# The second FFN rearranged, and the four weight sums of a tile made by VectorE

## What is computed

```python
D_MODEL = 1024
D_FF = ((8 * D_MODEL // 3 + 127) // 128) * 128   # 2816
def swiglu(x, w1, w3, w2):
    return (jax.nn.silu(x @ w1) * (x @ w3)) @ w2
x = x + 0.5 * rmsnorm(swiglu(rmsnorm(x, norm_g[4]), ffn2_w1, ffn2_w3, ffn2_w2), norm_g[5])
```

## Time and profile before

| what | us |
|---|---|
| median of 3 runs (lowest, highest) | 1102.76 (1102.58, 1103.33) |
| the profiled execution | 1100.35 |
| its span, first to last instruction | 1098.5 |
| PE busy | 1056.8 (96%) |
| DVE busy | 652.5 (59%) |
| ACT busy | 411.9 (37%) |
| POOL busy | 161.8 (15%) |

### The profile page before, as it was taken

The page is one execution under the profiler, slowest core; times in us unless marked ns, Lnnn a source line. Parts: engine busy times, 40 slices in busy tenths (PEclk is TensorE's granted clock), DMA queues, the critical chain, the costliest instruction groups (busy, mean ns, idle before and its releaser), DMA issues. The chain is left out here.

```text
span 1098.5 us, 21180 instructions
## 1 busy us (share of the span) xinstructions
PE 1056.8 (96%) x8729; PEld 1040.3 (95%) x8729; DVE 652.5 (59%) x1072; ACT 411.9 (37%) x650; POOL 161.8 (15%) x209
## 2 busy tenths in 40 slices
PE   8999999999999999999999999968999989999998
PEld 7999999999999999998999999968999989999997
DVE  6534433433333379784577778756883588368746
ACT  6322124222122345321447544433552255234432
POOL 0000716910000000520000000041320122022100
PEclk9999999999999999999999999979999999999999
DMA  7222322223222240223411152221323133312222
GB/s 255 78 95 77 96 77 96 82 90 92 81 77 95 72 140 22 75 78 119 138 59 58 40 175 88 96 67 49 115 93 111 30 116 123 94 41 91 82 73 82
DMA packets 31509, 99.40 MB, mean 90 GB/s; under 512 B 3780, under 2 KB 6212, under 8 KB 31304
## 3 DMA queue, kind: packets, MB, share of 16 engines
q1 hardware_dynamic: 31432, 98.33, 27.7%
HBM read 93.58 MB, written 4.74 MB: 89 GB/s over the span
## 5 line engine op out<-in xcount | busy, mean ns | idle before, releaser
L1304 DVE TENSOR_TENSOR wl<-raw,wh 128x1024 fp32r<-128x1024 f32 (+2 forms) x117 | 135.6, 1159 | 264.3 <-ACT wh L705 263.6
L705 ACT CAST wh<-raw 128x1024 fp32r<-128x1024 f32 (+2 forms) x117 | 114.3, 978 | 312.2 <-PE ps L2489 250.4
L2489 PE MATMUL ps<-xh,wh 128*128 128x272 f32 x1040 | 218.4, 291 | 13.1 <-DVE wl L1304 12.0
L2489 PE MATMUL ps<-xl,wh 128*128 128x272 f32 x1040 | 216.1, 289 | 0.0
L2489 PE MATMUL ps<-xh,wl 128*128 128x272 f32 x1040 | 215.6, 289 | 0.0
L2489 PEld LDWEIGHTS ps<-xh,wh 128*128 128x128 f32 x1040 | 164.1, 190 | 14.6 <-DVE wl L1304 12.9
L2489 PEld LDWEIGHTS ps<-xl,wh 128*128 128x128 f32 x1040 | 164.9, 190 | 0.0
L2489 PEld LDWEIGHTS ps<-xh,wl 128*128 128x128 f32 x1040 | 163.8, 190 | 0.0
L2720 PE MATMUL ps<-hh,wh 128*128 128x272 f32 x304 | 63.4, 290 | 7.1 <-DVE wl L1304 7.0
L2489 PE MATMUL ps<-hh,wh 128*128 128x272 f32 x304 | 63.2, 289 | 0.3 <-DVE hl L1325 0.3
L2720 PE MATMUL ps<-hl,wh 128*128 128x272 f32 x304 | 62.8, 288 | 0.0
(11 more groups left out here) (572 smaller groups left out, 2421.5 us busy)
## 6 DMA issues: line engine op xcount, KB each, us to landing
raw<-w SPq DMA_DIRECT2D x66, 512.0 KB, 3.6
pair<-w SPq DMA_DIRECT2D x36, 512.0 KB, 4.5
raw<-win SPq DMA_DIRECT2D x25, 512.0 KB, 3.7
raw<-w SPq DMA_DIRECT2D x32, 384.0 KB, 3.2
raw<-wout SPq DMA_DIRECT2D x8, 512.0 KB, 4.0
raw<-w SPq DMA_DIRECT2D x12, 256.0 KB, 2.7
o_yT<-x SPq DMA_DIRECT2D x8, 272.0 KB, 2.2
cs<-cT SPq DMA_DIRECT2D x4, 516.0 KB, 4.7
```

Of the source, the lines that this page charges most:

```text
L705: nc.scalar.copy(wh[par][:, 0:cols], raw[par][:, 0:cols]).then_inc(hi_done, 1)
L1304: V.tensor_tensor(wl[par][:, 0:cols], raw[par][:, 0:cols], wh[par][:, 0:cols].bitcast(F32), ALU.subtract).then_inc(split_done, 1)
L2489: last = mm(ps[:, bank + s, 0:HALF], w[:, kk * P:(kk + 1) * P], a[:, kk, s * HALF:(s + 1) * HALF], start=(kk == 0 and i == 0), stop=(kk == ...
```

## The change

Three things are rearranged and one moves between engines. (1) `sums` moves from the raw buffers to the unused fourth slots of `base_hi` and `base_lo`. With it d0 and d1 of a part are loaded in the part's first tile, and the sums and splits of the next part's first tile are made among the down units. The load of a pair now also waits for `g_lo`. (2) At the head, the split of u0+6 goes ahead of `normed`, that of u0+7 ahead of the forms, and forms and bases are spread over the down units of part 0, whose results ACT copies out (`down_copy`) in place of DVE. (3) PE does d1's last four k-tiles, not one, behind the last of d0. (4) All four sums of a tile are made by DVE (`sum_2`, `sum_4`); POOL's loop goes. In the tile loop DVE's `lo_4` and `lo_a22` move back, the latter behind `lo_3(j+1)`.

Cut to its core, indentation and renamed slices left out. The down units of part 0 get, on ACT, d2, copy 0, base 1, d3, copy 1, base 2, d4, copy 2, form 6, d5, copy 3, hi_3, hi_a22, d6, hi_4, copy 4, d7 and so on, and the like on DVE with `sum_13(0)`, `sum_2(0)` behind d4. In parts 1 and 2 DVE has sum_13, sum_2 ahead of d2 and sum_4, lo_3, lo_a22 behind it.

```diff
-        sums = sb("sums", [P, 4 * KHP], at=raw_at)
+        sums = sb("sums", [P, 2, KD * T], at=xh_at + 12 * FORM)
...
@@ SyncE: load_pair, ffn2
                     spe.wait_ge(a22_lo, j - 1)
+                    spe.wait_ge(g_lo, j - 1)
                     spe.wait_ge(s4_sum, j - 1)
...
                 load_pair(0)
-                load_pair(1)
...
-                    if p:
-                        for j in range(N6 * (p - 1), last):
-                            if j + 2 < NG:
-                                load_pair(j + 2)
-                        spe.wait_ge(s12_lo, last + 1)
-                        spe.wait_ge(s3_lo, last + 1)
+                    for j in range(N6 * (p - 1), N6 * p) if p else ():
+                        if j + 2 < NG:
+                            load_pair(j + 2)
+                        if j % N6 == 0:
+                            down(0)
+                            down(1)
+                    if p == 0:
                         down(0)
-                        spe.wait_ge(s4_lo, last + 1)
                         down(1)
-                        if last + 2 < NG:
-                            load_pair(last + 2)
-                    for m in range(2 if p else 0, KD):
+                        load_pair(1)
+                    for m in range(2, KD):
                         down(m)
@@ ScalarE: hi_form, new helpers, ffn2
-                act.wait_ge(form_raw, i + 1)
+                act.wait_ge(form_raw, min(i + 1, 4))
...
+            def hi_base(i, src):
+                act.wait_ge(unit_used, down_unit(0, 0) + 2)
+                nc.scalar.copy(base_hi_t[:, i], src).then_inc(form_hi, 1)
+            def down_copy(m):
+                act.wait_ge(unit_used, down_unit(0, m) + 3)
+                act.wait_ge(form_lo, (4, 4, 5, 5, 7, 7, 7, 7)[m])
+                nc.scalar.copy(halves(y[:, m, :]), pair(down_set(0) + 2 * (m % 2))).then_inc(y_evac, 1)
...
                 up_split(u0 + 6)
+                up_split(u0 + 7)
                 silu(hb + 2, 0)
                 hi_form(0, form_hi_t[:, 2], form_t3[:], 1.0)
-                hi_form(1, form_hi_t[:, 0], xn[:, 0, 1], 1.0)
-                hi_form(2, form_hi_t[:, 1], form_t24[:], -1.0)
-                hi_form(3, form_hi_t[:, 3], form_t24[:], 1.0)
-                up_split(u0 + 7)
                 hidden_hi(hb + 2, 0, 2)
...
                         down(0)
+                        hi_form(1, form_hi_t[:, 0], xn[:, 0, 1], 1.0)
                         silu(hb + 3, 1)
+                        hi_form(2, form_hi_t[:, 1], form_t24[:], -1.0)
                         down(1)
+                        hi_base(0, xn[:, 0, 0])
                         hidden_hi(hb + 3, 1, 3)
...
@@ ScalarE, tile loop of parts 1 to 3
-                            hi_4(j)
-                            hi_a22(j)
-                            if j > j0:
-                                silu_pair(j - 1)
-                            keep_p1(j)
...
+                        if j > j0:
+                            hi_4(j)
+                            silu_pair(j - 1)
+                        keep_p1(j)
...
+                            hi_g(j + 1)
+                        if j > j0:
                             hi_a22(j)
+                        keep_p5(j)
+                        keep_u2(j)
...
@@ VectorE: sums
+            def sum_2(j):
+                dve.wait_ge(s13_sum, j + 1)
+                V.tensor_tensor(s2_raw, s1_raw, pairs[j % 2][:, A11B], ALU.add).then_inc(s2_sum, 1)
+            def sum_4(j):
+                dve.wait_ge(s2_sum, j + 1)
+                if j:
+                    dve.wait_ge(s4_lo, j)
+                V.tensor_tensor(s4_raw, s2_raw, pairs[j % 2][:, A12B], ALU.add).then_inc(s4_sum, 1)
@@ VectorE: ffn2, head
                 hidden_lo(hb + 1, 1, 1)
+                up_lo(u0 + 6)
                 for kk in range(KD):
                     normed(kk)
-                up_lo(u0 + 6)
                 up_first(hb + 2, 0, u0 + 4)
-                lo_form(0, form_lo_t[2][:], form_t3[:], form_hi_t[:, 2], 1.0)
-                lo_form(1, form_lo_t[0][:], xn[:, 0, 1], form_hi_t[:, 0], 1.0)
-                lo_form(2, form_lo_t[1][:], form_t24[:], form_hi_t[:, 1], -1.0)
+                up_lo(u0 + 7)
                 scaled(hb + 2, 0)
-                lo_form(3, form_lo_t[3][:], form_t24[:], form_hi_t[:, 3], 1.0)
-                up_lo(u0 + 7)
...
                         down(0)
+                        lo_form(0, form_lo_t[2][:], form_t3[:], form_hi_t[:, 2], 1.0)
                         up_first(hb + 3, 1, u0 + 6)
                         scaled(hb + 3, 1)
+                        lo_form(1, form_lo_t[0][:], xn[:, 0, 1], form_hi_t[:, 0], 1.0)
                         gated(hb + 3, 1, u0 + 7)
+                        lo_form(2, form_lo_t[1][:], form_t24[:], form_hi_t[:, 1], -1.0)
                         down(1)
                         hidden_lo(hb + 3, 1, 3)
...
@@ VectorE, tile loop of parts 1 to 3
+                        if not last:
+                            sum_13(j + 1)
+                        if j > j0:
+                            c12(j - 1)
+                        if not last:
+                            sum_2(j + 1)
+                        c11(j)
+                        if j > j0:
                             lo_4(j)
+                        if not last:
+                            sum_4(j + 1)
+                        if j > j0:
+                            c22(j - 1)
+                        if last:
+                            down(0)
+                        else:
+                            lo_g(j + 1)
+                            lo_3(j + 1)
+                        if j > j0:
                             lo_a22(j)
+                        if last:
+                            down(1)
+                        else:
+                            lo_12(j + 1)
...
@@ GpSimd
-            for j in range(NG):
-                w = pairs[j % 2]
-                pool.wait_ge(s13_sum, j + 1)
...
-                G.tensor_tensor(sums[:, S2B], sums[:, S1B], w[:, A11B], ALU.add).then_inc(s2_sum, 1)
...
-                G.tensor_tensor(sums[:, S4B], sums[:, S2B], w[:, A12B], ALU.add).then_inc(s4_sum, 1)
@@ TensorE, end of the tile loop
                         enter_down(1)
-                        down(1, range(0, n - 1))
+                        down(1, range(0, 2))
                         down(0, range(n - 1, n))
-                        down(1, range(n - 1, n))
+                        down(1, range(2, n))
```

More of the change, by code:

```diff
@@ L308, in build @@
         N6 = PARTS2[1]
-        S2B, S4B, S1B, S3B = (slice(i * KHP, (i + 1) * KHP) for i in range(4))
+        s2_raw, s4_raw, s1_raw, s3_raw = (sums[:, b, i * KHP:(i + 1) * KHP] for b in range(2) for i in range(2))
         A21B, A22B, A11B, A12B = (slice(i * KHP, (i + 1) * KHP) for i in range(4))
@@ L316, in sums_12 @@
         def sums_12():
[L318 removed]
+            return sums[:, :, 0:KHP]
         def set_of(j):
@@ L931, in ffn2 @@
-                    if p < len(PARTS2) - 1:
-                        for m in range(2, KD):
+                        down(2)
+                        down_copy(0)
+                        hi_base(1, xn[:, 1, 0])
+                        down(3)
+                        down_copy(1)
+                        hi_base(2, xn[:, 1, 1])
+                        down(4)
+                        down_copy(2)
+                        hi_form(6, form_hi_t[:, 3], form_t24[:], 1.0)
+                        down(5)
@@ L933, in ffn2 @@
+                    silu_pair(j)
+                    hidden_hi(FT4 + j, 0, N6 - 1)
+                    if p < len(PARTS2) - 1:
+                        down(2)
+                        hi_3(N6 * p)
+                        hi_a22(N6 * p)
+                        down(3)
+                        hi_4(N6 * p)
+                        for m in range(4, KD):
                             down(m)
-                        hi_3(N6 * p)
                         hi_g(N6 * p)
@@ L1555, in ffn2 @@
-                    if p < len(PARTS2) - 1:
-                        for m in range(2, KD):
+                        lo_form(3, base_lo_t[:, 0], xn[:, 0, 0], base_hi_t[:, 0], 1.0)
+                        down(2)
+                        lo_form(4, base_lo_t[:, 1], xn[:, 1, 0], base_hi_t[:, 1], 1.0)
+                        down(3)
+                        lo_form(5, base_lo_t[:, 2], xn[:, 1, 1], base_hi_t[:, 2], 1.0)
+                        down(4)
+                        sum_13(0)
+                        sum_2(0)
@@ new lines, in ffn2 @@
+                        lo_form(6, form_lo_t[3][:], form_t24[:], form_hi_t[:, 3], 1.0)
+                        down(5)
+                        sum_4(0)
+                        lo_3(0)
+                        lo_a22(0)
+                        down(6)
+                        lo_4(0)
+                        down(7)
+                        lo_g(0)
+                        lo_12(0)
+                        continue
```

(42 more changed lines are left out.)

100 lines of the change are left out of this document (31 added, 69 removed).

## The result

The changed kernel takes 1090.71 us (median of 4 runs, 1089.30 to 1091.18), the kernel before 1102.67 beside it: ratio 0.9888, 95% interval 0.9871 to 0.9905. The forecast was 1091 us, the range 1075 to 1098. The profiled execution took 1090.49 us, its span is 1088.7.

What follows compares the result with a forecast made beforehand. PE, busy in 96% of the span, was taken as the bound, so only its idle time could be gained: 38.2 - 10.8 (head) - 15.6 (tile loops) = 11.8, about 12 us; 1102.76 - 12 = 1091 us, range 1075 to 1098.

Steps and rivals of the forecast that it cites:

- account of 38.2 us: PE's idle time to be had in the second FFN: 30.8 us listed waits, 4.0 restarts, 3.4 lower clock.
- The head: Idle of 0.5 ahead of u0+7, 2.4 ahead of d0, 5.9 inside d0; with clock and restarts 10.8 against 17.6 us.
- Down units of part 0, first tile, later parts: Waits go: 1.35 us ahead of d2, 1.7 at the first tile's entry, 6.4 ahead of the later parts' d2.
- cover of 3.0 us: Parts 1 to 3: four k-tiles of d1, 24 matmuls, just cover d2's chain of 2.9 us.
- The four sums: Tile loops: each moved sum costs DVE 0.6 us, 1.2 per tile; waits for c22 (7.4) and for lo_g go.
- The pair load: Tiles 2, 3, 4 of each part: late landings delay p6 and p4, 15.6 us in all against 14.3 before.
- fixed 2.4 us: Whole kernel: the profiled execution lies 2.4 us below the median of the runs.
- Rival C: Tile loops: the pair load is hidden, the loops' 15.6 us go, 1075; chance 0.17.
- D: Tile loops: each landing a microsecond later, +9, 1100; chance 0.06, half of it counted as no change.
- E: Tile loops: the half clock comes in, nine falls at 1.7 are 15.3 us, slower at 1106; chance 0.09.

Runs made afterwards that it cites:

- best: a22_early with the head reordered on DVE and ACT, up_first and hidden_lo ahead of forms, lo_form(2) behind the split of d2: 1067.63 us, 0.9690 to the kernel before.
- a22_early: The changed kernel with DVE's lo_a22(j) moved forward to right behind c12(j-1), and ACT's hi_a22(j) ahead of silu_pair(j-1): 1074.55 us.
- a22_mid: The changed kernel with DVE's lo_a22(j) moved forward one step, from behind to ahead of lo_3(j+1): 1084.96 us.
- a22_late: The changed kernel with DVE's lo_a22(j) moved back one step, behind lo_12(j+1): 1102.28 us.
- dve_sums_alone: The kernel before with only sums 2 and 4 made by DVE and POOL's loop gone, other orders kept: 1104.99 us, ratio 1.0021.
- pool_sums: The changed kernel with sums 2 and 4 back on POOL in its former loop, all other orders as changed: 1090.43 us.
- d1_undone: The changed kernel with PE's former order of d0 and d1, only one k-tile of d1 behind the last of d0: 1100.79 us.
- form2_late: The changed kernel with DVE's lo_form(2) moved from ahead of the split of d1 to behind hidden_lo(hb+3): 1086.87 us.
- d1_alone: The kernel before with only PE's new order, four k-tiles of d1 behind the last of d0: 1094.60 us, ratio 0.9930.

## Why the prediction was right, point by point

**What bounds the kernel, and the account of 38.2 us.** It held for this execution. best, which removes nearly all of it, is 33.1 us (1065.4 against 1098.5) shorter in span, and the changed kernel's waits can be read by the same account: 19.4 us listed, 18 x 0.25 in the loops, some 0.75 at the head, and the clock. What it left out is that the clock also falls behind the waits of 1.9 us in some executions, so that in the median the three waits ahead of d2 cost 8 to 10 us and not 6.4.

**The head.** Forecast 0.5, 2.4 and 5.9 us of idle; listed 0.3, 2.3 and 4.5. The mechanism was right in each step: both held splits, the `up_first` behind `lo_form(0)`, the last form of POOL served ahead of `hidden_lo`. The changed part began 1.3 us later in this execution than in before's (a silu of the head at 703.83 against 702.51); set against that, PE started d0 at the forecast time and went on inside it 0.3 us sooner than forecast. The last wait came out smaller (its delay is 4.9 less one matmul's 0.125, 4.8 against 5.9) above all because the clock had already fallen behind the wait ahead of d0: the 18 matmuls of d0 took 2.9 us instead of 2.3, inside a time in which PE would have waited anyway. The clock's loss behind it (16 matmuls in 3.7 us where about 30 fit, 1.8 us) was forecast as 1.7. In sum the head holds some 10.2 us, against 10.8. In a22_early, a22_mid and a22_late, where the first wait brought no fall, the last one is listed with 5.3.

The Trainium skill's rule of "SBUF — State Buffer" (section "Who interferes with whom") holds in the rows here: `hidden_lo`, with two SBUF inputs, took 3.00 us under POOL's fourth form. `gated` (L1521), with one input from PSUM, took its 0.72 while POOL's third form ran (722.51, POOL from 721.97 to 724.88).

**Down units of part 0, first tile, later parts.** Right: no wait ahead of d2 or in the first tile. The cover of 3.0 us for a chain of 2.9 held in all three parts.

**The four sums.** The price was right (0.6 from start to start); the sentence that the c22 and `lo_g` waits go because of it was wrong for the move alone. dve_sums_alone shows it: 1105.0, not less than before. What removed them in the changed kernel is the new order, since pool_sums without the move is just as fast; how much of it the early splits of a part's first tile did was not tested apart.

**The pair load.** Right in place and cause, and near in size. Forecast were nine tiles with 1.2 or 1.0 at p6 and 0.5 at p4; measured 7.4 in nine and 4.9 in nine, with the 0.16 of overlap 0.98 and 0.70 each. With restarts the loops hold 16.8 us against 15.6 forecast and 14.3 before. The period of a hit tile is 12.0 to 12.4 us, as forecast, but for the one of 13.4 behind the landing of 6.3. The `lo_a22` that frees the pair for tile 2 ends 10.0 us into its tile, as forecast, not ahead of 7.

The Trainium skill's page "DMA: Bandwidth & Descriptors" (section "Measured") gives 6.15 us for 1 MB, on GpSimd's queue. On SP's, eight of nine landings took 4.9 to 5.3 us from release on and one took 6.3, so the row of before (5.0) was the better figure.

**The total.** That it came out to within 0.3 us is luck: it was nearer than its terms deserve. In span the gain was 9.8 us, not 11.8 (1.3 of the difference lies ahead of the changed part), while in the median it was 12.0, because the fixed 2.4 us that I put between profiled execution and median became 0.2. Two errors of about 2 us cancelled. The term behind the second is that fixed difference, which is time at the lower clock in some executions and so changes with the waits. Rival C (loads hidden, 1075) is the kernel a22_early, 1074.55, and D's price (a microsecond per landing, +9) is near what a22_late shows for 1.15 us: +11.6. E, the clock in the loops, did not come in. But that 1.89 us left the clock up in before was no bound: single falls came behind waits of 1.8 us (dve_sums_alone) and 1.9 (d1_undone, pool_sums).

## What to carry to other kernels

Ask of each instruction that frees a buffer when the next load needs it, and put it as early in its engine's order as its data allow: here one subtraction of 0.68 us per tile, moved through four places, was worth 28 us. Waits that lie one behind the other in a chain are not separate gains; take the earlier one away alone and the later one can grow. Test each part of a large change by itself: here a new order of PE in two lines gives most of the time in the median, and the move of the sums gives nothing that can be measured. An instruction of another engine that waits on yours is started by your order, so put the one that starts a blocker of yours ahead of a stretch in which nobody needs you.

## What the runs showed of the hardware

DVE and POOL wait for each other by whole instructions, in turns, where the DVE instruction has two SBUF inputs. In the changed kernel and its variants each held DVE instruction ended 0.55 to 0.6 us (128x512 or 128x544) or 1.1 us (128x1024) behind the end of POOL's, and a POOL instruction that had asked during a DVE instruction was served before DVE's next (732.47 above).

The granted clock fell to 0.50, 1.2 GHz, behind waits of 2.3 us in before and in the changed kernel. It did not behind one of 2.3 in form2_late and in a22_early. It did behind one of 1.9 in d1_undone and one of 1.76 in dve_sums_alone, and did not behind two of 1.77 there. Of the nine waits at p6 in a22_late, 15.9 us in sum, one of 2.2 brought it down and one of 2.3 did not. So the length of the wait alone does not decide it, and what does isn't shown here. A fall in the loops or at the head cost 1.25 to 2.0 us, so that a wait of about 2 us is a cost of 2 or of 3.3 to 4 us.

Kernels that have several such waits spread more from run to run: dve_sums_alone 1100.9 to 1109.3 in 12 executions, d1_undone 1097.0 to 1104.5 in ten, against 1089.3 to 1091.2 in four for the changed kernel. Four are few; d1_alone, which has one of them left (2.3, at the head), spread from 1093.7 to 1096.3 in six.
